# A hybrid decoder step on one core: another tile order for the input projection, tiles kept on chip, the mixers beside it

## The chip, the cores and the metric

The kernel runs on one core of one Trainium2 chip. The metric is the device time of one execution in microseconds, the median of three runs. All data are fp32 in DRAM; the large products run on TensorE as three passes over fp32r operands, described below.

## The reference, cut to what matters

One layer of a decoder is computed for a prompt of 512 new positions and, with the same weights, for 8 sample sequences of one new token each, which attend to 4096 cached positions in 32 pages of 128.

```python
xn = rms_norm(x, norm1_g)
proj = xn @ w_in                      # 2048 -> 5128 columns: 40 tiles of 128, and 8 forget logits
u_pool, h_b, h_c, h_x, q, k, v, f_logit = split(proj)   # 4, 4, 4, 4, 8, 8, 8 tiles, 8 columns
y_pool = causal_pool_mix(u_pool)      # 4 groups: mean of 2, 4, 8, 16 rows, minus u, times pool_w
y_conv = h_b * causal_dwconv(h_c * h_x, conv_w)         # 3 taps
q, k = rms_norm(q, q_norm_g), rms_norm(k, k_norm_g)     # per head
logf = log_sigmoid(f_logit + b_f)
y_att = attn(q, k, v, logf)           # prompt: causal over 512; samples: 4096 cached + 1 own, paged
mix = concat([rms_norm(y_pool), rms_norm(y_conv), rms_norm(y_att)])
x = x + mix @ w_o
a, gate = split(rms_norm(x, norm2_g) @ w_up)            # 2048 -> 2 * 5632
x = x + (silu(causal_dwconv(a) + ffn_conv_b) * gate) @ w_down
```

Beside x it returns the new keys, values and log forget values, and the last rows of the pooling, convolution and FFN inputs. For the samples, every one of the 8 x 32 = 256 pages of keys and 256 pages of values (128 positions x 8 heads x 128, 0.524 MB each) is read once from the cache.

## The kernel before, in words

The five engines run programs of their own that are tied together by semaphores. Activations lie transposed, 16 tiles of 128 features x 520 columns (512 prompt positions and 8 samples). A product takes each operand as a high and a low part: `xh`, `xl` for the activations, `wh`, `wl` for the weights, and TensorE (PE) adds the three products xh·wh, xl·wh, xh·wl. Weights come in loads of 2 MB (256 columns, `t_wraw`, two buffers). ScalarE (ACT) copies a quarter of a load, called a chunk, into `wh` (`head(0, c)`, L1236), and VectorE (DVE) subtracts to get `wl` (`weight_rest`, L1639). Both have a ring of four chunks. One output tile of the input projection takes two chunks, each 48 matmuls of 260 columns.

The order of the middle of the program is written by hand as a list of slots. In each slot `s`, all five engines do what belongs to `s`; the engines are held together only by the semaphores. In the kernel before:

- Ahead of slot 2: the prompt is transposed and normed, the sample queries are computed from four weight loads through the same two `t_wraw` buffers (`sample_q`), and tile 0 is computed while its inputs are being normed.
- Slots 2 to 79 (`CHUNKS = 80`): one chunk of the input projection each. After every second slot ACT moves the finished tile from PSUM (L1339), keeps its 8 sample columns in `projS` and stores the rest to DRAM (`scr_proj`, L1342).
- Slots 80 to 141: no projection. The pooling mixer (`MIX0 = 81`), the convolution and then the eight prompt heads (`HEAD0 = 93`, a head every 6 slots, 7 stages each) read their tiles back from `scr_proj`. At the end the mixed outputs `ymix` are normed and split into `xh` and `xl` (`mix_pair`); tiles 8 to 15 of them at `TAIL` (142).
- Slots 143 to 174 (`OUT0 = 143`): the output projection, 32 chunks of 24 matmuls of 512 columns. Then the FFN: up and down projections in 11 groups, to the end of the program.

Beside this run the cache pages. SyncE (SP) issues the key pages into a ring of four (`kring`) and also all weight loads; GpSimd (POOL) issues the value pages into a ring of four (`vring`). DVE works off a key page with 8 custom multiply-and-add instructions (`key_page`, L1802). PE works off a value page with two fp32 matmuls of 512 columns (`value_page`). How many pages a slot has stands in `page_slots`: two keys in each slot (none in 82 to 93), values by a rate. 156 key and 56 value pages belong to the slots below 80, 100 and 112 to slots 80 to 142, none and 88 to the output projection. In a slot, DVE does the softmax steps of the samples, the stages of a prompt head, one key page, `weight_rest`, the mixers, and then the other key pages.

## Time and profile before

| | us |
|---|---|
| median of the runs | 2846.12 |
| lowest and highest of three | 2842.51, 2847.39 |
| span of the profiled execution, first to last instruction | 2839.4 |
| slots 2 to 17, as 92.8 to 201.9 of the span | 109.1 |
| slots 18 to 79, as 201.9 to 602.6 | 400.7 |
| slots 80 to 142 and the first two chunks of the output projection, as 602.6 to 1018 | 415.4 |
| the other 30 chunks, as 1018 to 1261.6 | 243.6 |
| from there to the end, the FFN above all | 1577.8 |

The profiled execution has no time of its own beside its span. The median of the runs is 6.7 us above the span; this is taken as what lies around it. The boundaries are read from the instructions that belong to the slots. The profile counts an engine as busy while an instruction runs; PEclk is the granted TensorE clock as a share of 2.4 GHz, and the DMA share is the mean busy share of the core's 16 DMA engines.

### The profile page before, as it was taken

Reading aid. Unit: us, or ns where it says so; the run is one execution under the profiler, and the core shown is the slowest. Engines: PE = TensorE matmul, PEld = TensorE weight load, DVE = VectorE, ACT = ScalarE, POOL = GpSimd, SP = SyncE. Lnnn points to the kernel's source line nnn. Section 1 sums busy time; section 2 is a strip of 40 time slices with the busy share of each in tenths; the row PEclk is TensorE's granted clock in tenths of the full one; section 3 lists DMA queues with packets and bytes.
Section 4 is the critical chain, followed back from the end, with each engine's and each line's share of the span. In section 5 each row is a group of like instructions: output and inputs, shape, how many; then the busy total and the mean of one; then the engine's idle time right before and its main releaser. Section 6 shows DMA issues by size and latency. Waiting matters only on the chain.

```text
span 2839.4 us, 50530 instructions
## 1 busy us (share of the span) xinstructions
PE 2651.8 (93%) x19656; PEld 2325.7 (82%) x19656; DVE 1426.1 (50%) x5629; ACT 732.9 (26%) x981; POOL 156.6 (6%) x317
## 2 busy tenths in 40 slices
PE   5899999977768699989999999999999999999998
PEld 3799989952333255659999999999999999999998
DVE  4787776765778732234434343434343434343433
ACT  4332212212333521133222222222222222222221
POOL 0100000012101122200000000000000000000000
PEclk7999999988867699989999999999999999999999
DMA  7689999998999887753222222222223222222221
GB/s 242 239 285 328 332 344 341 338 363 283 376 358 355 289 294 262 271 186 130 91 90 90 90 90 90 90 90 90 93 101 100 95 90 90 90 90 90 90 90 64
DMA packets 274531, 532.93 MB, mean 188 GB/s; under 512 B 16410, under 2 KB 177787, under 8 KB 272980
## 3 DMA queue, kind: packets, MB, share of 16 engines
q1 hardware_dynamic: 214573, 361.52, 37.1%
q0 software_dynamic: 39472, 142.46, 13.7%
q10 hardware_dynamic: 20247, 25.73, 2.5%
q8 instruction: 154, 2.52, 0.4%
q14 instruction: 85, 0.70, 0.1%
HBM read 503.94 MB, written 24.05 MB: 186 GB/s over the span
## 4 chain that ended last, share of the span: by engine, by line
PE 79%; DMA 7%; DVE 7%; issue 2%; ACT 2%; SPq 1%; ACTq 0%; POOL 0%; POOLq 0%; DVEq 0%
PE ps L711 78%; DVE t_work L1802 4%; DMA t_r<-in_cache_k 4%; DMA t_r<-in_cache_v 2%; DMA t_wraw<-in_w_in 1%; PE ps L714 1%; DVE t_xl L1639 0%; DVE t_stg L1695 0%; DVE t_nmax L1940 0%; SPq L584 0%; DVE t_wl L1639 0%; DVE t_work L1639 0%; DVE t_auxL L1947 0%; SPq L570 0%; ACT L1425 0%
## 5 line engine op out<-in xcount | busy, mean ns | idle before, releaser
L711 PE MATMUL ps<-t_xh,t_wh 128*128 128x260 f32 (+1 forms) x4352 | 949.1, 293 | 11.9 <-DVE t_xl L1639 11.8
L711 PE MATMUL ps<-t_xh,t_wl 128*128 128x260 f32 (+1 forms) x4352 | 935.7, 291 | 0.0
L711 PE MATMUL ps<-t_xl,t_wh 128*128 128x260 f32 (+1 forms) x4352 | 934.1, 290 | 0.0
L1639 DVE TENSOR_TENSOR t_wl<-t_wraw,t_wh 128x1024 fp32r<-128x1024 f32 x376 | 459.9, 1224 | 870.2 <-ACT t_wh L1236 870.2
L1236 ACT ACTIVATE t_wh<-t_wraw 128x1024 fp32r<-128x1024 f32 x376 | 398.1, 1060 | 1644.0 <-PE ps L711 1643.8
L711 PEld LDWEIGHTS ps<-t_xh,t_wh 128*128 128x128 f32 x4352 | 685.5, 190 | 94.2 <-issue 63.8
L711 PEld LDWEIGHTS ps<-t_xh,t_wl 128*128 128x128 f32 x4352 | 685.8, 189 | 11.8
L711 PEld LDWEIGHTS ps<-t_xl,t_wh 128*128 128x128 f32 x4352 | 685.4, 189 | 9.1
L1802 DVE CUSTOM_DVE_ANT_0 t_work<-t_r,t_work 128x128 f32<-128x128 f32 x2048 | 454.5, 285 | 154.9 <-DMA t_r<-in_cache_k 142.7
L711 PE MATMUL ps<-t_hh,t_wh 128*128 128x260 f32 x1408 | 285.8, 284 | 3.4 <-issue 3.4
L711 PE MATMUL ps<-t_hh,t_wl 128*128 128x260 f32 x1408 | 284.7, 284 | 0.0
L711 PE MATMUL ps<-t_hl,t_wh 128*128 128x260 f32 x1408 | 283.0, 282 | 0.0
L711 PE MATMUL ps<-t_r,t_work 128*8 128x512 f32 x1040 | 186.9, 670 | 67.2 <-DMA t_r<-in_cache_v 52.2
L1639 DVE TENSOR_TENSOR t_r<-ps,t_r 128x520 f32<-128x520 f32 (+1 forms) x184 | 128.5, 698 | 228.2 <-PE ps L711 228.2
L711 PEld LDWEIGHTS ps<-t_hh,t_wh 128*128 128x128 f32 x1408 | 218.3, 189 | 4.2 <-issue 3.7
L711 PEld LDWEIGHTS ps<-t_hl,t_wh 128*128 128x128 f32 x1408 | 217.3, 189 | 0.0
L711 PEld LDWEIGHTS ps<-t_hh,t_wl 128*128 128x128 f32 x1408 | 216.8, 189 | 0.0
L505 POOL DMA_DIRECT2D t_r<-in_cache_v x256 | 136.1, 532 | 959.2 <-PE ps L711 915.2
L1802 DVE DVE_READ_ACCUMULATOR2_ANT t_S<- 128x1 f32 x2048 | 164.6, 80 | 0.1
L711 PEld LDWEIGHTS ps<-t_r,t_work 128*8 128x8 f32 x1040 | 19.4, 88 | 148.7 <-DMA t_r<-in_cache_v 98.7
L520 POOL DMA_DIRECT2D out_ffn_sample<-t_aux x8 | 4.1, 518 | 1554.6 <-ACT t_aux L1236 1554.6
L1643 DVE SCALAR_TENSOR_TENSOR t_work<-t_work 128x8 f32<-128x8 f32 (+1 forms) x176 | 78.2, 486 | 3.1
(256 smaller groups left out, 1197.0 us busy)
## 6 DMA issues: line engine op xcount, KB each, us to landing
t_r<-in_cache_k SPq DMA_DIRECT2D x256, 512.0 KB, 7.2
t_r<-in_cache_v POOLq DMA_DIRECT2D x256, 512.0 KB, 6.5
t_wraw<-in_w_up SPq DMA_DIRECT2D x44, 2048.0 KB, 8.0
t_wraw<-in_w_in SPq DMA_DIRECT2D x22, 2048.0 KB, 11.6
t_wraw<-in_w_down SPq DMA_DIRECT2D x22, 2048.0 KB, 7.8
t_wraw<-in_w_o SPq DMA_DIRECT2D x11, 2048.0 KB, 12.2
scr_proj<-t_stg ACTq DMA_DIRECT2D x40, 256.0 KB, 5.5
t_aux<-scr_proj ACTq DMA_DIRECT2D x8, 768.0 KB, 18.4
```

Source lines behind the costliest of these rows:

```text
L505: pool.dma_start(vring[:, b, :], v_pages[bass.ds(g, 1), :, :].rearrange("a p n -> (a p) n")).then_inc(v_loaded[b], 16)
L520: pool.dma_start(o["ffn_sample"][0, b, 1, :].rearrange("(t n) -> t n", n=P), astrows[:, b, :]).then_inc(states_copied, 16)
L711: return pe.matmul(out, lhsT, rhs, start=start, stop=stop)
L714: return pe.transpose(out, in_, ident[0:n, 0:n])
L1236: return act.activation(out, in_, ACT.Copy)
L1639: return dve.tensor_tensor(out, in0, in1, op)
L1643: return dve.scalar_tensor_tensor(out, in0, scalar, in1, ALU.mult, ALU.add)
L1802: last = dve.tensor_tensor_reduce(out=junk[:, h * HD:(h + 1) * HD], in0=kring[:, p % RING, h * HD:(h + 1) * HD], in1=qcur[r % 2][:, h * HD ...
```

## The change

The projection's 40 tiles come in another order: the four pooling tiles, half of the convolution's (two groups of B, C, X), then for each pair of heads its q, k and v tiles, and last the other half of the convolution. A finished tile is not stored to DRAM. ACT copies it from PSUM to the place where its user reads it: `ub` for the pooling, and a ring of seven blocks of 512 columns for heads (`ring_blocks`). Tiles are computed half by half (`half_tile`): 260 columns over all 16 input tiles in the even slot, the other 260 in the odd one. The low part of the weights of the input projection is written over the raw weights (`t_wlr` on `t_wraw`), so a raw buffer is free only when PE is through with it; the load moves from SP's queue to ACT's (`load_raw`, issued in every slot with s % 4 = 3).

Pooling is in slots 10 to 17, half of the convolution in 19 and 21, and the prompt heads start at slot 32 (`HEAD0 = 32`) and end at slot 80, all beside the projection. The mixed outputs of these (13 tiles, `scr_y`) and two sums (`scr_m`) are stored to DRAM and read back at slot 80 (`load_y`). The output projection begins at slot 84 and takes its tiles in another order, 8 to 11 first. Between 79 and 84 lie the rest of the convolution, the norms of the mix and its 16 tiles.

There are three key pages in nearly each slot from 2 to 89, and two or four value pages from 18 on. Below slot 80 there are now 227 key and 154 value pages, in 80 to 83 there are 12 and 14, in the output projection 17 and 88. The sample queries' weights go to four buffers of their own; only the first quarter is used ahead of the norm, the others between the steps of tile 0.

On ACT, in the projection. Before, at two chunks and one finished tile (`t_stg` is the staging tile, `scr_proj` the DRAM copy):

```order
L1236 ACTIVATE t_wh<-t_wraw 128x1024 [waits weight_chunk_used,weights_loaded0]
L1236 ACTIVATE t_wh<-t_wraw 128x1024 [waits weight_chunk_used]
L1339 ACTIVATE t_stg<-ps 128x520 [waits sample_columns_kept,tile_spilled0,weight_chunk_used]
L1236 ACTIVATE t_projS<-t_stg 128x8 [waits accumulators0_free]
L1342 DMA scr_proj<-t_stg 128x512
```

After, at two slots in which a head is at its stages 4 and 5 (`t_work<-ps 128x260` and `128x252` are the two halves of a tile; `t_auxL` holds the head's probabilities):

```order
L1261 ACTIVATE t_work<-ps 128x260 [waits first_half_of_tile_full,head_scores_full]
L1480 ACTIVATE t_auxL,t_rsum<-ps,t_nmax 128x128 [waits head_max_ready]
L1480 ACTIVATE t_auxL,t_rsum<-ps,t_nmax 128x256
L1480 ACTIVATE t_auxL,t_rsum<-ps,t_nmax 128x384
L1480 ACTIVATE t_auxL,t_rsum<-ps,t_nmax 128x512
L1261 ACTIVATE t_wh<-t_wraw 128x1024 [waits weight_chunk_used]
L1261 ACTIVATE t_work<-ps 128x252 [waits weight_chunk_used]
L1261 ACTIVATE t_projS<-ps 128x8
L1400 DMA t_wraw<-in_w_in 128x16x256 [waits accumulators1_free,weight_chunk_used]
L1261 ACTIVATE t_wh<-t_wraw 128x1024 [waits weight_chunk_used]
L1261 ACTIVATE t_auxL<-ps 128x128 [waits head_probs_transposed,y_stored]
```

The store of the tile is gone; the head's work, with its waits for DVE and PE, stands in one program with the weight copies, and so does the weight load.

On DVE, between the projection and the output projection. Before, the last mixed tiles (`t_xl` is the low part of the output projection's input), at `TAIL`:

```order
L1955 SCALAR_TENSOR_TENSOR t_stg<-t_aux,t_par,t_work 128x512 [waits mix_rest_ready,mix_rstd_ready,mix_square_summed]
L1955 SCALAR_TENSOR_TENSOR t_stg<-t_aux,t_par,t_work 128x512 [waits mix_rest_ready,mix_rstd_ready]
L1639 TENSOR_TENSOR t_xl<-t_stg,t_xh 128x512 [waits mix_head_ready] x2
L1639 TENSOR_TENSOR t_wl<-t_wraw,t_wh 128x1024 [waits weight_head_ready] x2
L1821 TENSOR_REDUCE t_mx<-ps 8x1 [waits misc_bank_written]
```

After, the first mixed tiles, in slot 81:

```order
L1684 TENSOR_TENSOR t_aux<-t_aux 128x512 [waits conv_squares_loaded,mix_square_summed,mix_square_ready]
L1684 TENSOR_TENSOR t_aux<-t_aux 128x512 [waits mix_square_summed,mix_square_ready]
L2027 SCALAR_TENSOR_TENSOR t_stg<-t_aux,t_par 128x512 [waits y_loaded,pool_rstd_loaded]
L2027 SCALAR_TENSOR_TENSOR t_stg<-t_aux,t_par 128x512
L1684 TENSOR_TENSOR t_xl<-t_stg,t_xh 128x512 [waits mix_head_ready] x2
L2027 SCALAR_TENSOR_TENSOR t_stg<-t_aux,t_par 128x512 [waits mix_rest_ready] x2
```

All 16 mixed tiles are normed here after the change, and the first of them waits for the read back from DRAM; behind this wait stand DVE's key pages of slots 81 to 89 and the low parts of the first four chunks of the output weights.

The core of the diff:

```diff
+PAIRS = CHUNKS // 4
+QKV0 = 10
+HEAD0 = 32
 STAGES = 7
 HSTEP = 6
+OUT0 = CHUNKS + 4
+POOL0 = 10
+CONV_AT = (19, 21, CHUNKS, CHUNKS)
+def tile_order():
+    order = [T_U, T_U + 1, T_U + 2, T_U + 3] + [t + j for t in (T_B, T_C, T_X) for j in range(2)]
+    for p in range(HEADS // 2):
+        order += [t + 2 * p + j for t in (T_Q, T_K, T_V) for j in range(2)]
+    return order + [t + 2 + j for t in (T_B, T_C, T_X) for j in range(2)]
...
-            rate = ((2 if at % 2 == 0 else 0) if at < CHUNKS else (2 if at % 3 else 0) if HEAD0 < at < k_end[-1] else
-                    (4 if at % 3 else 2))
+            rate = (4 if at % 4 == 3 else 2) if at < CHUNKS else 4 if at < OUT0 or at % 3 else 2
...
+            def half_tile(t, b, pages):
+                pe.wait_ge(acc_free[b], t + 1)
+                for kt in range(KT):
+                    if b == 0 and kt % 8 == 0:
+                        pe.wait_ge(w_lo, 2 * t + kt // 8 + 1)
+                    last = tile_step(t, b, kt)
+                    if b == 0 and kt == KT - 1:
+                        last.then_inc(half_full, 1)
+                    if b == 1 and kt % 8 == 7:
+                        last.then_inc(w_used, 1)
+                    if kt == 5:
+                        value_pages(pages[:2])
+                    if kt == 11:
+                        value_pages(pages[2:])
...
-                act.activation(two(stg[:, s, :]), ps[:, 2 * s:2 * s + 2, 0:HALF], ACT.Copy).then_inc(acc_free[s], 1)
-                copy(projS[:, tile_at(t):tile_at(t) + 1, :], stg[:, s:s + 1, SEQ:T]).then_inc(tile_kept, 1)
-                act.dma_start(scr[tile_at(t)], stg[:, s, 0:SEQ]).then_inc(tile_spilled[s], 16)
+            def keep_half(t, b):
+                place = tile_place(t)
+                if b == 0:
+                    place_free(t)
+                    act.wait_ge(half_full, t + 1)
+                    copy(place[:, 0:HALF], ps[:, 0, 0:HALF]).then_inc(acc_free[0], 1)
+                    return
+                act.wait_ge(w_used, 4 + 2 * t + 2)
+                copy(place[:, HALF:SEQ], ps[:, 1, 0:SEQ - HALF])
+                copy(projS[:, TILES[t]:TILES[t] + 1, :], ps[:, 1:2, SEQ - HALF:HALF]).then_inc(acc_free[1], 1)
+            def load_raw(n):
+                act.wait_ge(w_used, 4 + 4 * (n - 1))
...
+                act.dma_start(wraw[:, n % 2, :].rearrange("p (k n) -> p k n", k=KT),
+                              source[:, :, col:col + 2 * P]).then_inc(w_loaded[n % 2], 16)
+            def load_y():
+                act.wait_ge(w_used, 4 + CHUNKS)
+                act.wait_ge(m_stored0, 16)
+                act.dma_start(msum[0], scrm[0]).then_inc(m_loaded0, 16)
+                act.wait_ge(m_stored1, 16)
+                act.dma_start(msum[1], scrm[1]).then_inc(m_loaded1, 16)
+                act.wait_ge(y_stored, 16 * 13)
+                act.dma_start(ymix[:, 0:6, 0:SEQ], scry[0:6].rearrange("k p t -> p k t")).then_inc(y_loaded, 16)
+                act.dma_start(ymix[:, 8:15, 0:SEQ], scry[6:13].rearrange("k p t -> p k t")).then_inc(y_loaded, 16)
...
+                if s == CHUNKS + 1:
+                    for n in range(13, 16):
+                        mix_sum(n)
+                    mix_pair(0)
+                    mix_pair(2)
+                if s == CHUNKS + 2:
                     dve.wait_ge(h_O, HEADS)
+                    dve.wait_ge(h_stored[1], 16 * HEADS)
                     weight_rest(0, CHUNKS)
                     weight_rest(0, CHUNKS + 1)
+                    weight_rest(0, CHUNKS + 2)
+                    weight_rest(0, CHUNKS + 3)
+                    dve.wait_ge(r_stored, 384)
+                    sample_squares(0, 8)
+                if s == CHUNKS + 3:
+                    for t in range(4, 16, 2):
+                        mix_pair(t)
```

## Rows read from the trace of the kernel before

**Rows 1.** Windows by stage: stretch, length, busy us of each engine, PEclk, DMA share, GB/s

```profile
core 0: us, PE busy (x) PEld busy (x) DVE busy (x) ACT busy (x) POOL busy (x), PEclk, DMA share, GB/s
92.80:201.90 109.10, 101.70 (x818) 101.26 (x817) 85.88 (x545) 33.87 (x47) 7.20 (x12) 0.95 0.85 295
201.90:602.60 400.70, 395.90 (x3223) 366.93 (x3222) 296.47 (x2103) 85.27 (x126) 29.68 (x56) 0.99 0.95 336
602.60:988.00 385.40, 275.43 (x1019) 116.21 (x1019) 277.08 (x1850) 132.86 (x237) 61.65 (x116) 0.76 0.92 335
1018.00:1261.60 243.60, 235.26 (x1230) 147.89 (x1230) 58.39 (x80) 46.32 (x63) 42.40 (x80) 0.98 0.69 239
```

**Rows 2.** The chain that ended last: start, length, what

```profile
40.86 3.65 PE ps L711 x32
44.52 8.42 DMA t_wraw<-in_w_in
...
1296.61 1471.92 PE ps L711 x12240
```

**Rows 3.** Timeline of ACT near 46 us: start, length, instruction, idle before

```profile
45.77 0.69 ACT L1269 ACTIVATE t_work<-ps,t_epsc 128x520 f32<-128x520 f32 x1 [10.66 <-PE ps L711]
```

**Rows 4.** DMA queues and issues in slots 18 to 79 (201.9 to 602.6)

```profile
q1 hardware_dynamic: 45471, 95.12, 67.9%
q0 software_dynamic: 7992, 29.13, 19.5%
...
t_r<-in_cache_k SPq DMA_DIRECT2D x126, 512.0 KB, 7.0
...
t_wraw<-in_w_in SPq DMA_DIRECT2D x13, 2048.0 KB, 11.6
```

**Rows 5.** Key pages' instructions on DVE (L1802) in slots 18 to 79: busy us

```profile
201.90:602.60 400.70, 223.99 (x2010) 0.99 0.95 336
```

**Rows 6.** Value pages' matmuls on PE in slots 18 to 79: busy us, mean ns

```profile
L711 PE MATMUL ps<-t_r,t_work 128*8 128x512 f32 x224 | 29.3, 594 | 0.0
```

**Rows 7.** Windows in the slots of the heads, with no projection

```profile
700.00:1002.00 302.00, 220.86 (x795) 101.25 (x794) 238.44 (x1673) 120.05 (x210) 38.30 (x72) 0.75 0.94 343
700.00:800.00 100.00, 67.10 (x245) 28.97 (x245) 73.73 (x560) 31.81 (x61) 12.71 (x24) 0.76 1.00 372
```

**Rows 8.** Groups on PE and DVE, 700 to 1002: busy us, mean ns, idle before

```profile
L711 PE MATMUL ps<-t_r,t_work 128*8 128x512 f32 x296 | 61.6, 760 | 39.3 <-DMA t_r<-in_cache_v 24.7 <-issue 9.0 <-ACT t_work L1236 5.5
L1802 DVE CUSTOM_DVE_ANT_0 t_work<-t_r,t_work 128x128 f32<-128x128 f32 x756 | 167.8, 285 | 38.7 <-DMA t_r<-in_cache_k 32.8 <-issue 0.2
L1955 DVE SCALAR_TENSOR_TENSOR t_stg<-t_aux,t_par,t_work 128x512 f32<-128x512 f32 x15 | 10.6, 744 | 0.3 <-ACT t_work L1463 0.3
L1639 DVE TENSOR_TENSOR t_xl<-t_stg,t_xh 128x512 fp32r<-128x512 f32 x14 | 9.2, 690 | 3.1 <-ACT t_xh L1236 2.8
```

**Rows 9.** Timeline of DVE: scans and biases of the pages' forget values, and a weight rest

```profile
127.66 1.22 DVE L1639 TENSOR_TENSOR t_wl<-t_wraw,t_wh 128x1024 fp32r<-128x1024 f32 x1
130.50 5.17 DVE L1766 TENSOR_TENSOR_SCAN t_work<-t_work 128x128 f32<-128x128 f32 x16
...
145.06 4.28 DVE L1776 TENSOR_SCALAR t_work<-t_work,t_tot 128x128 f32<-128x128 f32 x16
```

**Rows 10.** Timeline of PE at a wait at the end of slot 51

```profile
413.47 0.40 PE L711 MATMUL ps<-t_xl,t_wh 128*128 128x260 f32 x2
413.70 0.40 PE L711 MATMUL ps<-t_xh,t_wl 128*128 128x260 f32 x2
418.28 0.37 PE L714 MATMUL ps<-t_ident,t_mx 128*8 128x128 f32 x1 [4.18 <-DVE t_mx L1816]
...
418.98 0.64 PE L711 MATMUL ps<-t_xl,t_wh 128*128 128x260 f32 x2
419.41 0.64 PE L711 MATMUL ps<-t_xh,t_wl 128*128 128x260 f32 x2
```

**Rows 11.** Issues in slots 80 to 142: read back from DRAM on ACT's queue

```profile
t_aux<-scr_proj ACTq DMA_DIRECT2D x8, 768.0 KB, 18.4
```

More of the change, by code:

```diff
@@ L50, with ring_blocks @@
 CHUNKS = 80
-MIX0 = CHUNKS + 1
-HEAD0 = MIX0 + 12
+PAIRS = CHUNKS // 4
+QKV0 = 10
+HEAD0 = 32
 STAGES = 7
 HSTEP = 6
-TAIL = HEAD0 + (HEADS - 1) * HSTEP + STAGES
 KEY0 = 2
-K_RATE = 2
+OUT0 = CHUNKS + 4
+OUT_CHUNKS = 32
+SLOTS = OUT0 + OUT_CHUNKS
+POOL0 = 10
+CONV_AT = (19, 21, CHUNKS, CHUNKS)
+OWN_Q, OWN_K = 62, 69
+def tile_order():
[3 more added lines that the diff above has]
+    return order + [t + 2 + j for t in (T_B, T_C, T_X) for j in range(2)]
+def ring_blocks():
+    now, spare = [0, 1, 2, 3, 4, 5], 6
+    out = [list(now)]
+    for p in range(HEADS // 2):
+        now, spare = [spare, now[4], now[0], now[2], now[5], now[1]], now[3]
+        out.append(list(now))
+    return out
+TILES = tile_order()
+BLOCKS = ring_blocks()
+OUT_ORDER = [8, 9, 10, 11, 0, 1, 2, 3, 4, 5, 6, 7, 12, 13, 14, 15]
 def page_slots():
     keys, values, k_end, v_end = {}, {}, [], []
-    slots = [s for s in range(KEY0, TAIL) if not MIX0 < s <= HEAD0]
-    for n in range(DEC * PAGES):
-        keys.setdefault(slots[n // K_RATE], []).append(n)
+    at = KEY0
     for r in range(DEC):
-        k_end.append(slots[(PAGES * (r + 1) - 1) // K_RATE])
+        done = 0
+        while done < PAGES:
+            take = min(3, PAGES - done)
+            keys[at] = [r * PAGES + done + i for i in range(take)]
+            done += take
+            at += 1
+        k_end.append(at - 1)
     at = 0
@@ L221, in hybrid_layer_kernel @@
         rbs = [work[:, 7672:7672 + T], work[:, 1024:1024 + SEQ]]
-        msum = [work[:, SEQ * g:SEQ * (g + 1)] for g in range(3)]
-        t3p, t3o = work[:, 1600:1664], work[:, 1664:1728]
+        t3p, t3o = t3s[:, 0:64], t3s[:, 64:128]
         wtmp = work[:, 1728:1984]
@@ L799, in first_tiles, with first_tile @@
+            def first_tile():
+                for b in range(2):
+                    pe.wait_ge(acc_free[b], 1)
                 for kt in range(KT):
-                    half = kt // 8
-                    if before is not None:
-                        before(kt)
-                    pe.wait_ge(n_lo, normed + kt + 1)
+                    f_part(kt)
+                    pe.wait_ge(n_lo, kt + 1)
                     if kt % 8 == 0:
-                        pe.wait_ge(w_lo, g + 2 * us[-1] + half + 1)
@@ L806, in first_tiles @@
-                    for u in us:
-                        last = products(2 * u + half, u, kt)
-                        if u == 0 and kt == 7:
-                            last.then_inc(w_used, 1)
-                last.then_inc(w_used, 2 * len(us) - 1)
+                        pe.wait_ge(w_lo, kt // 8 + 1)
+                    for b in range(2):
+                        last = tile_step(0, b, kt)
+                        if b == 0 and kt == KT - 1:
+                            last.then_inc(half_full, 1)
@@ L819, in chunk @@
                 last.then_inc(w_used, 1)
-            def tile(t):
-                for half in range(2):
-                    chunk(0, 2 * t + half, t // 2 + 1, t, half)
             def biases_full(ns):
@@ L1176, in up @@
                     for half in range(2):
-                        chunk(i * 24 + 4 * R_F, c0 + 2 * u + half, i * 12 + (T_FF // 2 + u // 2 + 1), u, half)
+                        chunk(i * 24 + 4 * R_F, c0 + 2 * u + half, i * 12 + (ACC_F + u // 2 + 1), u, half)
             def down(i, c0, t0, after=None):
@@ L2053, in _ @@
-                if s == TAIL:
-                    mix_sum(15, 2)
+                if s == POOL0 + 2:
+                    dve.wait_ge(e_kept, 4)
+                    step(dve, seq, dve.memset(sums_pool, 0.0))
+                if pool_slot(s - 2) is not None:
+                    mix_sum(pool_slot(s - 2))
+                for g in range(CONV_T):
+                    if g < 2 and s == CONV_AT[g] + 2:
+                        mix_sum(4 + g)
+                    if s == CONV_AT[g]:
+                        conv_part(g)
```

892 lines of the change are left out of this document (443 added, 449 removed).

## The prediction

> **What bounds the kernel now.** I read the busy time by stage first. It cuts the span in two. From 1296.6 on PE runs without a gap, 12240 matmuls in 1471.9 us or 0.120 each [rows 2]; nothing there is touched. Ahead of it lie 1290 us in which several engines take turns. In slots 18 to 79 PE is busy 395.9 of 400.7 us and the DMA share is 0.95 [rows 1]: both are full. In slots 80 to 142 PE is busy 275 of 385 at a clock of 0.76, and the DMA share is still 0.92 [rows 1]. So the stage that the change takes apart, about 400 us without projection, is not empty time: the transfers of 212 pages fill it. What the reader is to see is that PE's free time there can be given to the projection, while DMA has little to give. The question is how long a slot is when projection, heads, three key pages and 2.5 value pages share it.
>
> **The start, to slot 2 (92.8).** The norm's logarithm sat idle 10.66 us behind a sample product that waited for its weights [rows 3], and then came 8.4 us for the next load [rows 2]. With four buffers of its own the norm goes first, and the first product of tile 0 some 14 us earlier (between 8 and 19). Three sample products now stand between the steps of tile 0, each 3.65 us at most [rows 2], half of that at the high clock: 5 to 11. Net I take -7 us (between -14 and +3): slot 2 at 86.
>
> **Slots 2 to 17 (109.1 before).** DVE sets this part. A key page is 16 of its records, 2010 of them in 224 us, so 1.78 us [rows 5]. 47 pages are 83.7; 16 weight rests at 1.22 are 19.5; scans and biases 9.5 [rows 9]; four pooling parts with 10 additions and some ten small steps each, at the 0.69 of a 512-column subtraction [rows 8], some 14, their squares' sums 3, the softmax steps 3. That is 133; with some 10 of waits, 143. The queries are stored and read back before the first page, some 8 more. PE needs 16 x 48 x 0.120 = 92, and DMA 47 pages, four weight loads and some 3 MB, 36 MB or about 100 at the stretch's best. So slot 17 ends at 86 + 151 = 237, between 222 and 250, against 201.9: the stage gets **42 us longer**, 35 with the start's 7.
>
> **Slots 18 to 79 (400.7 before).** Three costs per slot.
> DMA: 180 key and 154 value pages are 175.1 MB, 16 weight loads 33.6, and the rest (keys and values of the prompt, `scr_y`, queries) 11 MB. The value queue moved 29.13 MB in 0.195 x 400.7 us of all engines, 373 GB/s; taking the key pages at the same rate out of the other queue's 95.12 MB leaves 29.1 MB in 95 us, 306 GB/s for weights and the like [rows 4]. So 469 + 110 + 36 = 615 us at a full share, 9.9 per slot. The store and read back of the tiles, which this leaves out, was 20 MB.
> PE: the projection 48 x 0.120 = 5.77; 56 value pages took 29.3 us [rows 6], 2.5 of them 1.3; eight heads took the 220.9 - 61.6 us that were not value pages [rows 7, 8], 19.9 each at a clock of 0.75, so 15 at the full one, 2.5 per slot. Together 9.6 from slot 32, and 7.1 before.
> DVE: 2.9 pages 5.2, weight rest 1.2, a head with the softmax (238.4 less 168 for 94.5 pages and 20 for the norms [rows 7, 8], over eight) 6.3, 1.05 per slot: 7.5.
> PE and DMA are thus nearly equal, and neither can be used to the full. A key page waits for DVE, which from slot 32 waits for PE at a head's stages 4 and 5 and makes PE wait at 3 and 5. The nearest rows: the projection had a share of 0.95 with PE at 99% [rows 1], the head slots 0.94 over 302 us [rows 7], but there no engine was full beside DMA. I take a share of 0.93, 10.6 us a slot (10.1 before slot 32, 10.7 after): 14 x 10.1 + 48 x 10.7 = **655 us**, between 615 (full share) and 725 (below). Slot 79 ends at 892.
> The ceiling itself: the row reads 372 GB/s over 100 us at a share of 1.00 [rows 7].
> By the Trainium skill's page "DMA: Bandwidth & Descriptors", section "Where 436 GB/s comes from", the fabric's ceiling is 435 GB/s and the largest transfers on a single core read 425. By that the slot's 220 MB would be 517 us instead of 615 and PE alone would bind. No row here shows it at such a length; I give it a chance among the rivals.
>
> **From there to the end of the second output chunk (1018 before).** First the read back: 3.4 MB on ACT's queue, beside the key and value queues. 0.79 MB took 18.4 us there [rows 11], but the others stop soon when DVE waits: 20 to 30 us. DVE meanwhile has two convolution parts of some 4.5 us, and pages. Then in DVE's order four mixed tiles (a pair is 2 x 0.744 + 2 x 0.69 [rows 8] and a wait for ACT, 3.3), four weight rests 4.9, twelve mixed tiles 20, and ten key pages between them 18. 25 + 7 + 5 + 20 + 18 less what lies beside the read back, and one slot's rest, gives **68 us**, between 53 and 93; the chunk ends at 960. Before, it was 415 us after slot 79. This is the gain: 415.4 - 68 = 347, against 35 + 254 lost up to slot 79; at this point 58 are left (1018 - 960).
>
> **The other 30 chunks (243.6).** The same 88 value pages, but 17 key pages with 20 value pages in six slots, 19.4 MB, and weights and residuals of 5: 65 us at 372 GB/s against six slots of 8.1. Part is in the rings already: +12, between 0 and +25. The FFN is unchanged, 0.
>
> **The sum.** -7 + 42 (slots 2 to 17: 151 - 109) + 254 - 347 + 12 = -46. Against the span 2839.4 - 46 = 2793, and with the 6.7 us around it, **2800 us**.
>
> **Rivals.**
> *All of it overlaps (faster).* DMA keeps a share near 1 as in the row of 700 to 800 [rows 7]: 9.9 a slot, 615 instead of 655, 2760; with no loss in the output chunks 2748. For it: rings of eight pages in flight are 11 us of work. Against it: the 0.92 to 0.95 of all long stretches.
> *The ceiling is not 372.* If the transfers go at 425, PE binds: 14 x 8.3 + 48 x 9.6 = 577, 78 less than 655, 2722. Against it, a share of 1.00 at 372.
> *PE loses its clock (slower).* After an idle time of 4.18 us the matmul pairs came 0.43 us apart, before it 0.24 [rows 10], and the clock of the head slots was 0.75 with PE busy 73% [rows 7]. In the new slots PE waits inside a tile for value pages and behind a tile for the head's steps. If the clock there averages 0.80, PE's 9.6 become 12.0 and 48 slots cost 62 more: 2862. It decides from 11.7 us per head slot on, where the whole gain of 46 is gone. For it: DVE and PE wait for each other within a slot; against it, 0.99 in the projection at the same load, and 0.98 in the output chunks [rows 1].
> The Trainium skill, page "TensorE: Matmul & The Clock Gate", section "HAM oscillation — how this bites in real kernels", has a kernel whose compute between DMA waits is short and which falls to the low clock again and again; by it these slots would be at 1.2 GHz for much of their time. The row at 418 agrees on the fall, the projection's 0.99 speaks for long runs of matmuls saving it.
> *Head of line on ACT (slower still, or the same).* The weight load is now issued 1.5 slots before its first use, on a queue beside two full ones. It took 11.6 us on SP's queue [rows 4]; at a third of 354 GB/s (336 at a share of 0.95 [rows 1]) it would be 18, a slot and a half is 16. Two us at each of 16 loads are 32: 2832, no change that could be measured, or nearly.
>
> **How the numbers follow.** 0.2% is 5.7 us, about what a measurement of this kernel can tell from no change. The forecast (2775 to 2835) 0.45; all overlaps 0.18; the other ceiling 0.08; weights late 0.09, half of it within 0.2%; the lost clock 0.20. Faster 0.74, within 0.2% 0.07, slower 0.19. The range goes from near the second rival to past the lost clock: 2722 to 2870; below lie the cases in which several small terms help at once.
>
> **What would show it.** In the trace after: slot 17's tile kept near 237; 31 tiles later slot 79 at 892, so 21.1 us per tile; DMA share 0.93 and PEclk above 0.9 there; a gap of PE of 25 us or more after it that ends with the read back; the second output chunk at 960 and the first FFN matmul 46 us earlier than before. If the tiles come every 19 us the forecast was too careful about the coupling; if PEclk is below 0.85 and tiles take 23 or more, the lost clock is right. A page that costs DVE another time, now that the product is written over the key page itself, would make all of it wrong.

## The result, and the profile after

The changed kernel takes 2857.73 us (median of 12 runs, 2850.56 to 2864.78) against 2846.44 for the kernel before (12 runs on the same chip). The ratio is 1.0042, with a 95% interval of 1.0030 to 1.0054: slower by 0.4%, where the prediction said 2800 and faster. Its profiled span is 2856.5 us, 17.1 more than before.

The busy time by stage of the changed kernel, cut at tile 0 kept, slot 17, slot 79, the end of the third output chunk and the end of the last one; the columns are those of [rows 1]:

```profile
core 0: us, PE busy (x) PEld busy (x) DVE busy (x) ACT busy (x) POOL busy (x), PEclk, DMA share, GB/s
91.06:227.48 136.42, 115.69 (x821) 110.46 (x819) 116.74 (x763) 32.42 (x60) 8.25 (x16) 0.87 0.81 277
227.48:916.06 688.58, 594.75 (x4198) 478.47 (x4199) 462.90 (x3200) 197.72 (x361) 81.42 (x154) 0.92 0.87 317
...
916.06:1018.85 102.79, 52.55 (x241) 24.16 (x243) 76.80 (x399) 29.60 (x45) 21.85 (x43) 0.72 0.79 291
1018.85:1271.80 252.95, 236.26 (x1214) 147.79 (x1214) 75.90 (x241) 45.77 (x62) 44.51 (x85) 0.97 0.76 266
```

The same cuts in the kernel before, from slot 79 on. The prediction called 1018 the end of the second output chunk; counted by its matmuls it is the end of the third (1017.3), and the second ends at 1009.3:

```profile
602.60:1017.25 414.65, 303.07 (x1152) 130.66 (x1156) 295.48 (x1877) 144.24 (x251) 66.94 (x126) 0.77 0.93 336
1017.25:1259.30 242.05, 233.71 (x1212) 147.08 (x1211) 57.24 (x78) 45.99 (x62) 42.40 (x80) 0.98 0.70 242
```

The large shift happened as planned: the 415 us after slot 79 became 103. It was paid with 288 us in slots 18 to 79, where the prediction had 254. There PE is idle for 94 of 688.6 us and the DMA share is 0.87, not 0.93. So neither is full, and DVE is busy for 463 of these us; something makes them wait. What ACT waited for in that stretch (total, times, longest), and the issues of the large transfers (count, size, median us from issue to landing):

```profile
ACT t_wh L1261 <- DMA t_wraw<-in_w_in: 163.6, 13, 25.8
```

```profile
t_r<-in_cache_k SPq DMA_DIRECT2D x184, 512.0 KB, 7.2
t_r<-in_cache_v POOLq DMA_DIRECT2D x154, 512.0 KB, 7.8
t_wraw<-in_w_in ACTq DMA_DIRECT2D x14, 2048.0 KB, 26.0
```

A weight load takes 26.0 us on ACT's queue; it took 11.6 on SyncE's [rows 4]. One such place on ACT's timeline, in slots 47 to 49 (start, length, instruction, idle before):

```profile
559.11 0.38 ACTq L1400 DMA_DIRECT2D t_wraw<-in_w_in  x1
559.54 1.06 ACT L1261 ACTIVATE t_wh<-t_wraw 128x1024 fp32r<-128x1024 f32 x1 [0.54 <-ACT t_projS L1261]
561.15 0.60 ACT L1261 ACTIVATE t_auxL<-ps 128x512 f32<-128x512 f32 x1 [0.55 <-PE ps L737]
561.78 15.83 ACTq L1452 DMA_DIRECT2D out_k_prompt<-t_auxL  x1
577.71 0.39 ACT L1261 ACTIVATE t_auxL<-ps 128x260 f32<-128x260 f32 x1 [15.96 <-issue]
...
583.79 1.06 ACT L1261 ACTIVATE t_wh<-t_wraw 128x1024 fp32r<-128x1024 f32 x1 [3.65 <-DMA t_wraw<-in_w_in]
```

Two things are to be seen. The load issued at 559.1 is there only at 583.8, 24.7 us later. And the issue of a 256 KB store 2.7 us behind it does not take 0.4 us, as an issue does, but 15.8: ACT cannot copy, exponentiate or free a PSUM bank meanwhile. So there are two suspects, the late load and the held issue, and a third possibility, a common limit: that the slots are as long as PE, DVE and DMA make them together, and ACT merely shows the waiting.

The stretch behind slot 79, on ACT, DVE and PE of the changed kernel (one view each):

```profile
916.62 0.38 ACTq L1400 DMA_DIRECT2D t_wraw<-in_w_o  x1
...
917.30 8.17 ACTq L1502 DMA_DIRECT2D t_aux<-scr_m  x1
...
925.51 1.64 ACTq L1504 DMA_DIRECT2D t_aux<-scr_m  x1
927.47 1.32 ACTq L1506 DMA_DIRECT2D t_aux<-scr_y  x1
928.82 11.51 ACTq L1507 DMA_DIRECT2D t_aux<-scr_y  x1
940.37 0.60 ACT L1261 ACTIVATE t_aux<-ps 128x512 f32<-128x512 f32 x1 [20.96 <-issue]
```

```profile
954.02 1.42 DVE L2027 SCALAR_TENSOR_TENSOR t_stg<-t_aux,t_par 128x512 f32<-128x512 f32 x2 [6.41 <-DMA t_aux<-scr_y]
```

```profile
992.81 0.40 PE L734 MATMUL ps<-t_xh,t_wl 128*128 128x512 f32 x1
1007.18 1.90 PE L734 MATMUL ps<-t_wraw,t_work 128*8 128x256 f32 x16 [13.98 <-issue]
```

The read back was issued from 917.3 to 940.3 behind the weight load and was there at 954.0. And PE, done with the second output chunk at 993.2, did nothing for 14.0 us. The view names no releaser (`issue`), but by the program PE needed the sample norms for `sample_out(0)`, and on DVE their sums (L2067, at 1004.6) stood behind six key pages of 1.78 us.

### The profile page after: what moved, and what is told of

It is laid out like the page before. It is cut to its first block, busy times and chain, and to the rows that moved or that the text cites. A ratio compares the mean times of both kernels' runs of the same rounds, so it can differ in the third digit from the quotient of the medians.

```text
span 2856.5 us, 50766 instructions
## 1 busy us (share of the span) xinstructions
PE 2618.9 (92%) x19729; PEld 2343.0 (82%) x19729; DVE 1426.0 (50%) x5630; ACT 733.0 (26%) x1029; POOL 169.5 (6%) x343
## 4 chain that ended last, share of the span: by engine, by line
PE 74%; DMA 12%; DVE 7%; issue 3%; ACT 2%; ACTq 1%; POOL 0%; POOLq 0%; DVEq 0%; SPq 0%
PE ps L734 73%; DMA t_wraw<-in_w_in 8%; DVE t_r L1855 3%; DMA t_r<-in_cache_v 2%; PE ps L737 1%; ACTq L1452 1%; DMA t_wraw<-in_w_o 1%; DMA t_aux<-scr_y 1%; DVE t_xl L1684 1%; ACT t_wh L1261 1%; DVE t_work L1684 1%; DMA t_r<-in_cache_k 1%; DVE t_stg L1740 0%; DVE t_auxL L1684 0%; DVE t_wlr L1684 0%
## 5 line engine op out<-in xcount | busy, mean ns | idle before, releaser
L734 PE MATMUL ps<-t_xh,t_wh 128*128 128x260 f32 (+1 forms) x4352 | 1078.5, 299 | 52.2 <-ACT t_projS L1261 31.2
L734 PE MATMUL ps<-t_xl,t_wh 128*128 128x260 f32 (+1 forms) x4352 | 1051.3, 293 | 0.0
L734 PEld LDWEIGHTS ps<-t_xh,t_wh 128*128 128x128 f32 x4352 | 743.6, 193 | 186.8 <-issue 119.0
L1684 DVE TENSOR_TENSOR t_wl<-t_wraw,t_wh 128x1024 fp32r<-128x1024 f32 x296 | 362.5, 1226 | 825.4 <-ACT t_wh L1261 825.4
L734 PEld LDWEIGHTS ps<-t_xl,t_wh 128*128 128x128 f32 x4352 | 742.5, 192 | 10.2 <-issue 1.2
L734 PE MATMUL ps<-t_xh,t_wl 128*128 128x260 f32 (+1 forms) x3072 | 677.7, 294 | 0.0
L734 PEld LDWEIGHTS ps<-t_xh,t_wl 128*128 128x128 f32 x3072 | 488.0, 190 | 11.9
L1855 DVE CUSTOM_DVE_ANT_0 t_r<-t_r,t_work 128x128 f32<-128x128 f32 x2048 | 454.8, 286 | 47.0 <-DMA t_r<-in_cache_k 31.5
L734 PE MATMUL ps<-t_xh,t_wlr 128*128 128x260 f32 x1280 | 373.3, 292 | 0.0
L734 PEld LDWEIGHTS ps<-t_xh,t_wlr 128*128 128x128 f32 x1280 | 254.6, 199 | 0.0
L734 PE MATMUL ps<-t_r,t_work 128*8 128x512 f32 x1040 | 160.4, 621 | 58.7 <-ACT t_work L1261 24.7
L1684 DVE TENSOR_TENSOR t_wlr<-t_wraw,t_wh 128x1024 fp32r<-128x1024 f32 x80 | 97.5, 1220 | 137.8 <-ACT t_wh L1261 137.8
```

The source lines that it names most:

```text
L734: return pe.matmul(out, lhsT, rhs, start=start, stop=stop)
L1684: return dve.tensor_tensor(out, in0, in1, op)
L1855: last = dve.tensor_tensor_reduce(out=kring[:, p % RING, h * HD:(h + 1) * HD], in0=kring[:, p % RING, h * HD:(h + 1) * HD], in1=qcur[r % 2 ...
```

## Experiments

Each kernel was run on the chip beside the kernel before. "Slots 18 to 79" and "tail" (slot 79 to the end of the third output chunk) are read from the one traced execution of each kernel; the changed kernel has 688.6 and 102.8. The kernel before had medians of 2841.3 to 2846.4 beside these runs, so a few us between two rows of the table are better taken from the ratios.

| run | median us | ratio to before, 95% interval | slots 18 to 79 | tail |
|---|---|---|---|---|
| the change | 2857.7 | 1.0042 (1.0030 to 1.0054) | 688.6 | 102.8 |
| loads_on_sp | 2803.0 | 0.9858 (0.9841 to 0.9874) | 633.1 | 105.1 |
| heads_late | 2806.1 | 0.9866 (0.9849 to 0.9882) | 638.1 | 101.8 |
| stores_on_sp | 2850.2 | 1.0020 (1.0010 to 1.0031) | 673.7 | 103.5 |
| y_before_load | 2847.9 | 1.0019 (1.0007 to 1.0030) | 683.5 | 96.8 |
| wide_rows | 2774.7, one run | none | 613.0 | 101.6 |
| both_fixes | 2805.1 | 0.9864 (0.9833 to 0.9895) | 638.9 | 105.1 |
| out_load_later | 2793.8 | 0.9835 (0.9804 to 0.9866) | 632.7 | 97.6 |
| sums_first | 2805.7 | 0.9865 (0.9834 to 0.9896) | 634.5 | 91.4 |
| sums_and_load_first | 2792.6 | 0.9819 (0.9795 to 0.9843) | 633.3 | 93.6 |
| late_heads_tail | 2792.2 | 0.9824 (0.9797 to 0.9851) | 635.9 | 90.3 |
| spread_loads | 2780.0 | 0.9768 (0.9743 to 0.9794) | 622.8 | 99.1 |
| spread_and_tail | 2760.9 | 0.9702 (0.9681 to 0.9723) | 622.8 | 75.5 |

### Is the late load the cause?

**loads_on_sp**: `load_raw` leaves ACT's program, SyncE issues it between key pages.

```diff
-                    if s % 4 == 3:
-                        load_raw((s - 3) // 4 + 2)
...
                     page(kring, k_pages, k_loaded, k_used, g, *divmod(n, PAGES))
+                    if i == 0 and s % 4 == 0 and s <= CHUNKS:
+                        load_tiles(s // 4 + 1)
```

> The 2 MB weight loads of tiles 4 and on are issued by SyncE between a slot's first and second key page, as soon as PE is through with the buffer, instead of by ACT; nothing else is changed. Theory A (loads late and ACT held): a load lands after 11 to 15 us instead of 24.5, ACT's 164 us of waits for it fall below 60, no DMA issue of ACT takes over 2 us, slots 18 to 79 take 640 to 665 us instead of 688.6, and the read back of the mixed outputs is not held up either (10 to 20 us); in all 35 to 55 us faster than the changed kernel, so 2803 to 2823. Theory B (the slots are as long as DMA, PE and DVE make them together, and the load is only where ACT happens to wait): the load lands earlier but the keys behind it later, DVE waits for key pages instead (15 us now, then over 60), and slots 18 to 79 stay within 10 us of 688; 2845 to 2858.

**heads_late**: the load stays where it is; its first user comes a slot later, on ACT and on DVE.

```diff
+                if 2 < s < CHUNKS and s % 4 == 2:
+                    head(0, s + 2)
+                    head(0, s + 3)
                 if s < CHUNKS and s % 2:
-                    head(0, s + 3)
+                    if s == 1 or s % 4 == 3:
+                        head(0, s + 3)
...
```

> The loads stay on ACT's queue. The first two of each four chunks are copied into the high part one slot later (slot 4j+2 instead of 4j+1), and DVE's low parts with them, so a load has 2.5 slots until ACT waits for it instead of 1.5. Only the lateness is taken away, not ACT's held issues. Theory A (late landing is the larger part): ACT's 164 us of waits for loads fall below 50 and slots 18 to 79 take 655 to 670; 2825 to 2840. Theory A' (held issues are the larger part: 15.0, 10.6, 9.6, 11.1, 15.8 and 15.6 us in these slots): within 10 us of the changed kernel. Theory B (common limit): the same.

Both moved the end by 52 to 55 us (50 and 52 by the ratios). heads_late gained more than any of its expectations had. The stretch of slots 18 to 79 of heads_late, its load, and ACT's waits for loads:

```profile
220.47:858.57 638.10, 585.32 (x4201) 473.31 (x4202) 462.61 (x3188) 197.08 (x363) 82.04 (x155) 0.94 0.93 342
```

```profile
t_wraw<-in_w_in ACTq DMA_DIRECT2D x14, 2048.0 KB, 26.7
```

```profile
ACT t_wh L1261 <- DMA t_wraw<-in_w_in: 28.5, 3, 14.9
```

The load is as late as ever (26.7 us) and costs little any more, since ACT seldom stands at it. ACT's issues are still held in this run: in slots 18 to 79 five of them took 10.2 to 16.0 us, against six of 9.6 to 15.8 in the changed kernel, and all 44 issues together 90 us against 98. One of the five:

```profile
519.48 16.04 ACTq L1452 DMA_DIRECT2D out_k_prompt<-t_auxL  x1
```

So the cause is that 26 us from issue to landing do not fit into the 1.5 slots between issue and first use. heads_late makes the distance longer and loads_on_sp the landing shorter, and the one gives nearly what the other does, though loads_on_sp also ends the held issues (29 issues, 11 us, none over 0.5). ACT's waits for loads fell from 163.6 us to 28.5 in heads_late, and 50 of these 135 us were gained in the slots. The rival of a common limit is out, for its slots would have stayed at 688. The same in loads_on_sp, where the first use is as early as before, ACT's waits for loads are 52.5 us, and a part of the waiting went to another engine:

```profile
t_wraw<-in_w_in SPq DMA_DIRECT2D x14, 2048.0 KB, 15.6
```

```profile
DVE t_r L1861 <- DMA t_r<-in_cache_k: 113.5, 28, 10.2
```

The load lands after 15.6 us, above the 11 to 15 expected, and DVE now waits 113.5 us for the key pages behind it (15.0 before the edit). This half of theory B came true, without its consequence: the slots are 633.1 us long, below the 640 to 665 of theory A. The read back did not come in 10 to 20 us, as theory A had it, but in 30.5.

**both_fixes**: the two together.

> Loads issued by SyncE and the first two chunks of four copied one slot later. Each alone gave slots 18 to 79 of 633 and 638 us. If the late load was the whole excess there, the two together find nothing more: 2795 to 2806. If each left a rest of its own (58 us of ACT's waits for loads remained with the one, DVE waited 69 us for ACT's copies with the other), slots 18 to 79 fall to 615 to 625, near the 615 us of DMA at a full share: 2780 to 2792.

Nothing more was found: 638.9 and 2805, with only 2.6 us of waits for loads left on ACT. The two remove one and the same cause.

### Is it the held issue?

**stores_on_sp**: only the prompt's stores leave ACT.

```diff
-                act.dma_start(o[("v_prompt", "k_prompt")[n]][0, 0].rearrange("(j p) h d -> p j h d", p=P)[:, :, h, :],
-                              row.rearrange("p (j d) -> p j d", j=4)).then_inc(h_stored[n], 16)
...
+                    if i == 1:
+                        head_stores(s - 1)
```

> The stores of the prompt's keys and values and of the heads' mixed outputs are issued by SyncE one slot later instead of by ACT; the weight loads stay on ACT's queue. Only ACT's held issues of these stores are taken away (58 us in 16 issues of keys and values, most of it in four), not the lateness of the loads. Theory A': slots 18 to 79 get 25 to 45 us shorter, 2813 to 2833. Theory A with the lateness as the larger part: 5 to 20 us, 2838 to 2853, because PE had work while ACT was held. Theory B: within 5 us.

7.5 us at the end (6 by the ratios), 15 in the slots. ACT's waits for loads did not shrink (175.8 us in 13): where ACT is no longer held by a store, it stands at the load instead. The two stores of sums (`scr_m`) were still issued by ACT and held it for 14.6 and 8.8 us. The held issue is real, but the load was late anyway; it is the smaller part.

### Why is the load so late beside the pages?

**wide_rows**: each load fetches 4 x 1024 columns instead of 16 x 256, the same 2 MB. The products of tiles 4 to 39 and of two output tiles are those of other weights.

```diff
-                              source[:, :, col:col + 2 * P]).then_inc(w_loaded[n % 2], 16)
+                              source[:, 4 * (n % 4):4 * (n % 4) + 4, col:col + 1024]).then_inc(w_loaded[n % 2], 16)
```

> The changed kernel with its loads on ACT's queue as they are, but each 2 MB load fetches 4 x 1024 columns of the weights (rows of 4 KB, as the pages have) instead of 16 x 256 (rows of 1 KB). The products of tiles 4 to 39 and of two output tiles are then those of other weights; every instruction, size and wait is the same. If a load is late because the DMA engines take turns between the queues row by row, so that a queue of 1 KB rows beside two of 4 KB rows gets far less than a third, it now lands 13 to 19 us after its issue instead of 24.5, ACT's waits for it fall from 164 us below 70, and slots 18 to 79 take 635 to 655 us: 2803 to 2825. If only the number of queues and the total matter, it lands within 2 us of 24.5 and the time is within 10 us of the changed kernel's 2857.

The queues of the changed kernel in slots 18 to 79 (packets, MB, share of 16 engines), and ACT's queue and load in this run:

```profile
q1 hardware_dynamic: 27137, 98.78, 38.8%
q0 software_dynamic: 21869, 79.66, 30.8%
q10 hardware_dynamic: 41152, 38.82, 16.8%
```

```profile
221.20:834.20 613.00, 581.31 (x4204) 464.27 (x4205) 465.34 (x3209) 198.49 (x361) 82.40 (x156) 0.96 0.94 357
```

```profile
q10 hardware_dynamic: 18112, 38.82, 16.5%
```

```profile
t_wraw<-in_w_in ACTq DMA_DIRECT2D x14, 2048.0 KB, 19.6
```

In the changed kernel a packet of ACT's queue (q10) holds 38.82 MB / 41152 = 943 bytes, one of the key pages' queue (q1) 98.78 / 27137 = 3640. With rows of 4 KB ACT's packets hold 2143 bytes, and the load lands after 19.6 us instead of 26.0, so by the row and not by equal shares of the queues; 19.6 is a little above the 13 to 19 expected. ACT still waits 75.8 us for loads, and yet the slots (613.0) and the time (2774.7, in one run) are far below the 635 to 655 and 2803 to 2825 expected. Second, the same bytes took less of the DMA engines' time: 38.82 MB in 0.168 x 688.58 us are 336 GB/s, in 0.165 x 613.0 us they are 384. For the 33.6 MB of loads that is 12.5 us, half of the 25 us by which this run's slots are below those of heads_late. The other half has no measured cause. One difference is that no issue of ACT in these slots took 1 us here, while five took 10 us and more in heads_late. The Trainium skill, page "DMA: Bandwidth & Descriptors", section "Queues, rings and completion order", says that each DMA engine takes turns between the queues that have work, one packet at a time. The late landing on the queue with the small packets (943 bytes beside 3640) agrees with it; the run cannot tell the turns from the faster rows by itself, since both changed together.

### Can the load be fitted in?

**spread_loads**: SyncE issues four pieces of 0.5 MB between the key pages, first use a slot later, the output load in slots 82 and 83.

```diff
+                sp.dma_start(wraw[:, n % 2, :].rearrange("p (k n) -> p k n", k=KT)[:, 4 * j:4 * j + 4, :],
+                             source[:, 4 * j:4 * j + 4, col:col + 2 * P]).then_inc(w_loaded[n % 2], 16)
```

> SyncE issues each weight load of tiles 4 to 39 in four pieces of 0.5 MB, one behind each of four successive key pages (three in slot 4j, one in 4j+1), the first two chunks of four are copied one slot later, and the load of the output chunks 4 to 7 goes in the same way in slots 82 and 83. If the 119 us that DVE waited for key pages with both fixes come from the 2 MB that stand ahead of them in SyncE's queue, they fall below 50, slots 18 to 79 take 612 to 628 us instead of 639, and the kernel 2768 to 2785. If they come from the total of bytes in rows of 1 KB (342 GB/s there, 359 with rows of 4 KB), slots 18 to 79 stay at 630 to 640 and the kernel, with the gain of the later output load of some 9 us, at 2790 to 2800.

```profile
221.30:844.10 622.80, 585.28 (x4204) 472.15 (x4205) 462.36 (x3190) 197.78 (x363) 81.98 (x155) 0.95 0.96 352
```

```profile
DVE t_r L1877 <- DMA t_r<-in_cache_k: 109.3, 57, 4.6
```

622.8 and 2780, as expected, but not for the reason given: DVE still waits 109 us for keys, where "below 50" was expected. Only the longest single wait fell, from 10.2 us to 4.6. That PE has enough in hand to cover the short waits is a guess which no run isolates. DMA is now at 0.96, PE at 585 of 623.

### The tail

**y_before_load**: at slot 80 ACT issues the read back first, then the load.

```diff
                 if s == CHUNKS:
                     load_y()
                 for h, stage in head_stages(s):
                     prompt_head(h, stage)
+                if s == CHUNKS:
+                    load_raw(R_O + 1)
```

> Only the order on ACT at slot 80 is changed: the read back of the mixed outputs is issued before the 2 MB weight load of the next output tiles instead of behind it, and the load comes behind ACT's work of that slot. If the read back was late because it stood behind the load in ACT's queue, it lands 15 to 22 us after its issue instead of at 954 (37 us after 916.6), ACT's 21 us without work go, the first mixed tile comes 12 to 20 us earlier, and 8 to 18 of that reach the end: 2840 to 2850. If it was late because the three queues share the bandwidth of the pages, it lands no earlier than 948 and the time is within 5 us of the changed kernel.

The second part of it landed 29.6 us after its issue at 912.8, at 942.5, which is 32.4 us after slot 79's end instead of 37.9. Neither expectation fits: ACT's order is worth 5.5 us, and the read back takes 30 with no weight load ahead of it. The weight load, now behind it, held ACT for 10.1 us in its turn. The tail gained 6 us; slots 18 to 79, which the edit does not touch, differ by 5 as well. By the ratios the edit gained 6.5 us and not the 10 of the medians.

**out_load_later**: loads_on_sp, with the load of output chunks 4 to 7 in SyncE's slot 82.

```diff
-                    if i == 0 and s % 4 == 0 and s <= CHUNKS:
+                    if i == 0 and s % 4 == 0 and s < CHUNKS:
                         load_tiles(s // 4 + 1)
+                    if i == 0 and s == CHUNKS + 2:
+                        load_tiles(R_O + 1)
```

> Loads on SyncE as in the first run, and the weight load of the output chunks 4 to 7 is issued in SyncE's slot 82 instead of 80, so it does not stand ahead of the key pages, nor beside the read back of the mixed outputs; it is first used in slot 84. In the run with loads on SyncE DVE had no key page for 20 us behind this load and the mixed outputs landed 30.5 us after their issue. If that order is what makes the stretch from slot 79 to the end of the third output chunk 105 us, it falls to 82 to 92 and the kernel takes 2782 to 2793. If the stretch is bound by the pages and the read back together whatever their order, it stays within 4 us and the load is missed in slot 84 instead: 2798 to 2808.

97.6 instead of 82 to 92: 7.5 us gained and not 13 to 23. DVE had its pages, but the read back again took 30.0 us (860.2 to 890.2), and that now ends the wait. **late_heads_tail** therefore lets the first mixed tiles start with the first 1.5 MB:

```diff
-                    dve.wait_ge(y_loaded, 32)
+                    dve.wait_ge(y_loaded, 16)
...
+                if t == 6:
+                    dve.wait_ge(q_stored, 32)
```

> The loads stay on ACT's queue with the first two chunks copied one slot later, as in the second run (2806, slots 18 to 79 in 638 us), and two edits at the tail: the load of the output chunks 4 to 7 is issued by SyncE in slot 82, and the mixed tiles 0 to 3 wait only for the first 1.5 MB of the read back. With SyncE's loads the first of these gave 10 us; the stretch from slot 79 to the end of the third output chunk was 102 us. If the read back's 30 us are what starts the mixed tiles late, the first one comes 10 to 15 us after the first issue earlier than before and the stretch falls to 80 to 90: 2784 to 2795. If DVE's key pages of slots 81 to 83 stand in the way anyway, it falls by less than 5 us beyond the 10: 2793 to 2798.

The tail is 90.3 us, 11.5 below that of heads_late and just outside the 80 to 90 expected; PE's 14.0 us for the sample norms are still in it. **sums_first** (on loads_on_sp) puts them ahead of the pages:

```diff
+                if s == CHUNKS + 3:
+                    kp, held = kp[:1], kp[1:]
+                if s == OUT0:
+                    kp, held = [], held + kp
...
+                if s == OUT0:
+                    sample_sums(0, 2, Y_TOT)
+                    sample_scale(0, 2, Y_RS)
+                    for n in held:
+                        key_page(*n)
```

> Loads on SyncE as in the first run, and on DVE the sample norm's sums of slot 85 stand ahead of the six key pages of slots 83 and 84 instead of behind them; the pages follow. PE waited 14.0 us for these sums after the second output chunk. If this wait is real cost, it falls below 4 us, the stretch from slot 79 to the end of the third output chunk gets 8 to 11 us shorter and the kernel takes 2791 to 2797. If the pages now late hold up PE or SyncE afterwards (the residual loads wait for the last key page), the gain is given back in the output chunks: 2800 to 2806.

The wait fell to 3.2 us, the tail to 91.4, and the kernel was not faster. The 29 chunks behind took 274.0 us instead of 251.9. SyncE's queue in loads_on_sp and here, at slot 90 (the last row of each holds two loads, of which the first, of slot 90, was issued at the start of the row, and its issue took 12.6 and 11.8 us):

```profile
996.82 0.52 SPq L671 DMA_DIRECT2D t_pr<-scr_x  x1
997.44 28.08 SPq L610 DMA_DIRECT2D t_wraw<-in_w_o  x2
```

```profile
1005.88 1.84 SPq L671 DMA_DIRECT2D t_pr<-scr_x  x1
1007.82 18.11 SPq L610 DMA_DIRECT2D t_wraw<-in_w_o  x2
```

The last key page now ends later, SyncE waits for it ahead of the residuals, and the output weights stand behind both in its program. They are issued 10 us later, and counted from the end of the third chunk 58.1 us behind it instead of 36.3, which is the 22 us lost. ACT waits 46.4 us for these weights instead of 17.5. The gain was turned into the same fault at another place. **sums_and_load_first** only moves these loads ahead in SyncE's program:

```diff
+                n, late = divmod(s - OUT0 + 6, 4)
+                if late == 0 and 2 <= n < 8:
+                    load_raw(R_O + n, n % 2, w_o_v, OUT_ORDER[2 * n] * P)
                 res = scrx.rearrange("k p t -> p k t")
```

> As the run with the sample sums ahead of the six key pages, which won 13 us up to the third output chunk and lost 22 behind it; now SyncE also issues the output weight loads of slots 86 and 90 ahead of the key pages and the residual loads of these slots. If the 22 us were lost because the load of slot 90 came 10 us later behind the last key page (issued at 1007.8, landed 24.9 us later), they come back at least in half: 2785 to 2796. If they were lost to the key pages or the residuals themselves, the time stays at 2800 to 2808.

2792.6: 13 us came back, the chunks behind take 256.6. **spread_and_tail** has all of it, spread_loads, the read back in two steps, the sums and the loads ahead of the pages:

> All of it together: loads in four pieces between the key pages, first chunks copied one slot later, read back in two steps, output load in slots 82 and 83, sample sums ahead of six key pages, output loads ahead of the key pages. If the gains add up (slots 18 to 79 at 612 to 628, the stretch to the third output chunk at 75 to 85, the 30 chunks behind it no longer than 252): 2745 to 2770. If the late pages and residuals take the tail's gain back: 2775 to 2790.

```profile
844.80:920.30 75.50, 51.05 (x232) 23.00 (x229) 68.54 (x339) 29.09 (x43) 21.41 (x42) 0.77 0.92 346
920.30:1175.50 255.20, 237.48 (x1215) 148.40 (x1214) 85.19 (x309) 45.99 (x62) 44.54 (x85) 0.97 0.78 277
```

2760.9 us in five runs, 3.0% below the kernel before (2.8 to 3.2) and 97 us below the change as it came. The gains add up: 66 in slots 18 to 79, 27 in the tail, 6 ahead of slot 18, less 2 in the chunks behind, which took 255.2 us where no more than 252 were expected.

## Why the prediction was wrong, point by point

Its sum, term by term, up to the first FFN matmul (1296.6 before, 1314.0 after), against the kernel before:

| term | predicted | measured |
|---|---|---|
| start and slots 2 to 17 | +35 | +25.6 (227.5 for 201.9) |
| slots 18 to 79 | +254 | +287.9 (688.6 for 400.7) |
| slot 79 to the second output chunk | -347 | -329.6 (77.1 for 406.7) |
| third output chunk | in the line above | +17.7 (25.7 for 8.0) |
| the 29 chunks behind | +12 | +10.9 |
| norms between them and the FFN | 0 | +4.9 |
| sum | -46 | +17.4 |

The sum missed by 63 us, and two terms of equal size are nearly all of it: 34 in slots 18 to 79 and 35 in the tail. The start was 9 us better than its term, and the norms ahead of the FFN, put at nothing, cost 5.

- **The start** held: tile 0 was kept at 91.1 for 98.3 us, the 7 us. Slots 2 to 17 were 10 us shorter than its 151; DVE was busy for 117 of 136 us, where its sum had 133 of work.
- **The step that failed** first is that the sum has no term for the late weight load: it stands only as the rival "Head of line on ACT", at 2 us a load and a chance of 0.09. The rival's mechanism was right, with its place and its condition (a slot and a half, 16 us). It let the load have a third of the bandwidth, 18 us, so 2 us late at 16 loads. The load took 26.0, some 10 us over the budget, and ACT waited 163.6 us in 13 waits. The rival also let every us of lateness reach the end; with 160 us it would have said 2960. The edits that took this wait away gave 50 to 55 us. So it had the lateness too small by a factor of five and the part that reaches the end too large by one of three. The signs were in [rows 4]: q1, with the weight loads in it, has 95.12 MB in 45471 packets, 2.1 KB each, and the value pages 3.6. The weights' rows were shorter, and the 11.6 us were measured where the load stood in line with the key pages and not on a queue beside them.
- **The 11.6 us were no floor and no measure** for a third queue. Even on SyncE's queue beside these pages it is 15.6.
- **Slots 18 to 79 otherwise** were not too cheap: without the late load they take 633 to 638 us against its 655, with a share of 0.93 to 0.95, near the 0.93 predicted. PE's costs per slot nearly hold: 585 busy, where 14 x 7.1 + 48 x 9.6 is 560.
- **The tail** is the second step that failed. Its 68 us end at the second chunk, which took 77.1, inside its 53 to 93. But it was set against 415.4 up to the third chunk instead of 406.7 up to the second, and the third chunk, in which PE waits 14.0 us for sums behind six key pages, had no term. The prediction named the weights and tiles behind DVE's pages but not the sample norms. The boundary (8.7 us) and the third chunk (17.7) are 26 of the 35 us by which the tail missed, and the second chunk's 9 the rest.
- **The read back** was put at 20 to 30 us; its second part took 22 to 34 in the runs, and 12 more for ACT's held issues in the changed kernel. This the prediction had not: it priced the transfer and not its issue.
- **All overlaps** and **the other ceiling** (2748 to 2760 and 2722) did not come. The queue of the value pages moved 376 GB/s of its engines' time, near the 373 of the sum, and ACT's queue 336, where the sum had 306 for weights. Up to 384 are seen with 4 KB rows on ACT's queue, and none of the stages had 425.
- **The lost clock** did not come either, though its time (2862) is the nearest to the result. The granted clock was 0.92 in slots 18 to 79 against the 0.80 it assumed. Without the late loads it is 0.94, and PE's busy time only 9.4 us less. That its number came near is luck.

So the range held the time and the sign was wrong. heads_late, the change with one wait moved, lands at 2806, near the forecast of 2800; but that is in part luck: there a stage 17 us cheaper than predicted stands against a tail 34 us dearer.

## What to carry to other kernels

Where a transfer moves to another queue, ask first how long it is from its issue to its first use, and price its landing by the packets it has beside those of the other queues, not by its bytes. If it is late, look at the first use as well as at the queue: the copies of the first two of each four chunks, put one slot later, gave 52 us, nearly the 55 of the other queue, and no transfer was moved. And in a program with one order per engine, look behind each step that you delay: the wait comes back at the next load that stands behind it.

## What the runs showed of the hardware

- **An issue can hold its engine.** A 256 KB store on ACT's queue took 15.8 us to issue 2.7 us behind a 2 MB load of 1 KB rows, and 0.38 us where the queue was free. In slots 18 to 79 six issues took 9.6 to 15.8 us, each with such a load on its way ahead of it. Not every issue behind a load is held: two others, 5.2 and 12.5 us behind one, took 1.5 and 3.4 us, a third in slots 2 to 17, 4.4 us behind one, took 0.35, and in wide_rows, where the loads have 4 KB rows, none in these slots took 1 us. SyncE is held as well: a 2 MB load behind 3 MB of residuals took 12.6 us to issue in loads_on_sp. What decides it was not tested. The Trainium skill, page "DMA: Bandwidth & Descriptors", section "Issuing engines are not separate DMA queues", calls the issue time usually small next to the transfer. Here it was 15.8 us, while in both_fixes, with no load in ACT's queue, such stores from `t_auxL` had landed 6.3 us after their issue (median of four). The measurement decides.
- **Row length counted twice here**, in one run. 2 MB in rows of 4 KB landed 19.6 us after its issue beside two busy queues, in rows of 1 KB 26.0, and ACT's queue moved 384 GB/s of its engines' time instead of 336.
- **The sum of an engine's waits is not their cost.** In both_fixes DVE waited 119.1 us for keys in 30 waits of up to 10.2 us, in spread_loads 109.3 in 57 of up to 4.6. The sums are nearly equal; the slots took 638.9 and 622.8 us, with the pieces and the later output load as the only differences. Whether the length of the single wait decides it, or the DMA share, which rose from 0.94 to 0.96, the runs do not show.
